# A four-layer transformer kernel: two late weight tiles placed elsewhere, a tile split at another place, and the first attention units and token halves taken in another order

## The reference

```python
def hybrid_layer(x, ...):                       # twice
    h = rms_norm(x, norm_mix)
    proj = h @ w_in                             # queries, keys, values of four mixers, gates
    ys = [nsa_mixer(...), stick_breaking_mixer(...), gla_mixer(...), forgetting_mixer(...)]
    branch = jnp.einsum('bsnc,ncd->bsnd', ys, w_branch)
    mixed = jnp.sum(gates * branch, axis=2)
    x = x + mixed @ w_out
    return x + jnp.square(jax.nn.relu(rms_norm(x, norm_ff) @ w_ff1)) @ w_ff2

def second_block(x, c, ctx, c_ctx, ...):
    for i in range(2):                          # i = 0: GQA, 512 tokens; i = 1: MLA, 256 tokens
        sh_a, sc_a, g_a, sh_m, sc_m, g_m = split(silu(c) @ w_ada[i] + b_ada[i], 6)   # and for c_ctx
        y = mixer_i(x * (1 + sc_a) + sh_a, ...)          # 16 heads, softmax attention
        x = layer_norm(alpha * x + g_a * y, ...)
        x = layer_norm(alpha * x + g_m * sq_relu_mlp(x * (1 + sc_m) + sh_m, w1, w2), ...)
```

## Time and profile before

| | |
|---|---|
| three runs | 2367.37, 2374.55 and 2376.17 us; median 2374.55 |
| profiled execution | 2367.38 us, of which 2365.6 us are the span from first to last instruction |
| mean granted clock | 0.979 |
| TensorE busy | 2235.9 us, 95% of the span |
| VectorE, ScalarE, GpSimd busy | 1239.0, 691.1 and 479.0 us |
| TensorE not busy | 129.7 us of the span (2365.6 - 2235.9) |

### The profile page before, as it was taken

One profiled execution on the slowest core, in us unless ns is written; L12 is line 12 of the kernel. 1 busy time (PEld: TensorE's weight loads), 2 busy tenths in 40 slices (PEclk: granted clock), 3 DMA queues, 4 the chain that ended last, 5 costly groups with the idle time before them and its releaser, 6 DMA issues.

```text
span 2365.6 us, 33139 instructions
## 1 busy us (share of the span) xinstructions
PE 2235.9 (95%) x13928; PEld 1805.5 (76%) x13928; DVE 1239.0 (52%) x1689; ACT 691.1 (29%) x1530; POOL 479.0 (20%) x259
## 2 busy tenths in 40 slices
PE   7999999999999999999999897889999998998998
PEld 7998788799888977887998644447888884555887
DVE  5675436764445744367653226664443443465666
ACT  2224453122012244532220357522112112262211
POOL 2221112243312211122432000101111110102332
PEclk9999999999999999999999898999999999999999
DMA  7634665564365355655646311022223222202551
GB/s 229 215 136 149 215 250 161 189 231 186 125 183 215 108 183 215 245 161 201 226 179 214 110 47 42 1 71 89 84 95 107 73 81 87 88 26 77 197 197 65
DMA packets 210120, 340.13 MB, mean 144 GB/s; under 512 B 46475, under 2 KB 78198, under 8 KB 209846
## 3 DMA queue, kind: packets, MB, share of 16 engines
q1 hardware_dynamic: 208880, 334.50, 40.8%
q0 software_dynamic: 944, 3.47, 0.4%
q10 hardware_dynamic: 150, 0.04, 0.0%
HBM read 335.90 MB, written 2.10 MB: 143 GB/s over the span
## 4 chain that ended last, share of the span: by engine, by line
PE 57%; ACT 4%; DVE 3%; issue 1%; DVEq 0%; ACTq 0%
PE bank L2057 15%; PE bank L268 13%; PE bank L270 12%; PE bank L269 12%; PE bank L635 3%; PE bank L2060 2%; ACT work L2378 1%; DVE ring_low L256 1%; ACT work L2294 1%; ACT work L1093 1%; DVE cos L2572 1%; PE bank L638 0%; ACT L1093 0%; ACT work L2303 0%; PE bank L928 0%
## 5 line engine op out<-in xcount | busy, mean ns | idle before, releaser
L269 PE MATMUL bank<-hT_high,ring_low 128*128 128x256 f32 (+1 forms) x2032 | 604.0, 297 | 0.0
L269 PEld LDWEIGHTS bank<-hT_high,ring_low 128*128 128x128 f32 x2032 | 387.8, 191 | 12.4 <-issue 0.5
L249 POOL CAST ring_high<-ring 128x2048 fp32r<-128x2048 f32 (+2 forms) x108 | 203.7, 1887 | 712.3 <-PE bank L270 649.8
L256 DVE TENSOR_TENSOR ring_low<-ring,ring_high 128x2048 fp32r<-128x2048 f32 (+2 forms) x108 | 239.0, 2215 | 131.8 <-POOL ring_high L249 131.6
L268 PE MATMUL bank<-hT_low,ring_high 128*128 128x256 f32 (+1 forms) x1008 | 293.5, 291 | 15.4 <-DVE ring_low L256 7.9
L270 PE MATMUL bank<-hT_high,ring_high 128*128 128x256 f32 (+1 forms) x1008 | 285.7, 283 | 0.0
L249 POOL CAST half_high<-ring 128x2048 fp32r<-128x2048 f32 x64 | 128.6, 2013 | 675.4 <-PE bank L270 469.9
L268 PE MATMUL bank<-ring_low,hidden_high 128*128 128x512 f32 x640 | 254.0, 397 | 0.0
L1093 ACT ACTIVATE work<-bank 128x512 f32<-128x512 f32 (+10 forms) x268 | 121.3, 476 | 377.7 <-PE bank L270 320.1
L268 PEld LDWEIGHTS bank<-hT_low,ring_high 128*128 128x128 f32 (+1 forms) x1008 | 190.6, 189 | 26.5 <-issue 17.0
L256 DVE TENSOR_TENSOR ring_low<-ring,half_high 128x2048 fp32r<-128x2048 f32 x64 | 152.7, 2391 | 99.7 <-POOL half_high L249 99.2
(11 more groups left out here) (236 smaller groups left out, 4482.0 us busy)
## 6 DMA issues: line engine op xcount, KB each, us to landing
ring<-w_ff SPq DMA_DIRECT2D x32, 2048.0 KB, 8.0
ring<-mlp_w SPq DMA_DIRECT2D x32, 2048.0 KB, 7.9
ring<-w_in SPq DMA_DIRECT2D x30, 2048.0 KB, 8.1
ring<-w_ada SPq DMA_DIRECT2D x24, 2048.0 KB, 7.7
ring<-w_branch SPq DMA_DIRECT2D x24, 512.0 KB, 6.2
ring<-w_in SPq DMA_DIRECT2D x32, 256.0 KB, 4.2
ring<-w_out SPq DMA_DIRECT2D x4, 2048.0 KB, 7.5
ring<-gqa_w_qkv SPq DMA_DIRECT2D x3, 2048.0 KB, 7.7
```

The lines of the kernel that those rows point to most:

```text
L249: nc.gpsimd.tensor_copy(self.high(i), self.part(i, False)).then_inc(self.high_made, 1)
L256: nc.vector.tensor_tensor(self.part(i, True), self.part(i, False), self.high(i).bitcast(F32), ALU.subtract)\
L269: nc.tensor.matmul(out, a[1], b[0], start=False, stop=False)
```

## The change

It has six parts. No arithmetic is added or removed; the products, their operands and their sizes stay, except that the first two `up` chunks of the GQA layer are taken as two halves of 256 tokens.

```diff
+    late_tiles = Carver(gates.rearrange("p a b -> p (a b)")).take(2, KD, 512)
...
-    tiles += [ada_tile(n) for n in ada_late]
...
-    slots += [0, 2, 1, 0, 2, 1, 0, 2]
-    feed = [1, 3, 0, 2]
-    slots += [feed[n % N_SLOTS] for n in range(len(tiles) - len(slots))]
-    W = Weights(sem, "w", chip["ring"], slots, tiles, prev.held, {"up1": done("wo11")})
+    slots += [0, 2, 1, 0, 2, 1]
+    slots += [0, 2, 1, 3, 0, 2, 3, 1, 0, 3, 2, 1, 0, 3, 2, 1]
+    W = Weights(sem, "w", chip["ring"], slots, tiles, prev.held, {"up3": done("wo11")})
...
-        W.load(sp, back_at)
+        W.load(sp, back_at, W.order["up0"] + 1)
+        sp.wait_ge(mixed_whole, KD // 2)
+        for at, n in enumerate(ada_late):
+            sp.dma_start(late_tiles[:, at], w_ada[:, :, 512 * n:512 * n + 512]).then_inc(wk1_in, 16)
+        W.load(sp, W.order["up1"])
...
         Y.make_low(nc, dve, OUT_CUT + 3)
+        X.make_low(nc, dve, 0, 1)
         add_out(1, 0)
         norm(0, TT + 1, xn)
         add_out(1, 1)
         norm(1, TT + 2, xn)
         for c in range(2):
             low_bits("yT", ROW_FF, hT_high[1], c)
-        X.make_low(nc, dve, 0, 1, 2, 3)
+        X.make_low(nc, dve, 2, 3)
```

```diff
-    tiles = [*q_tiles, cmp_tile, in_tile("kwg", KS0 + 256, 280, "vwg"), in_tile("kvs", KS0, 256, "vs"),
+    tiles = [*q_tiles, cmp_tile, kk_tile, vv_tile,
...
         if l > 0:
-            Y.make_low(nc, dve, 0, 1)
+            Y.make_low(nc, dve, 0)
```

The copy of `fc`. ACT takes it between the two tiles of the GLA output:

```diff
         for t in range(TT):
+            if t == 1:
+                ps = PROJ.arrived(act, "fc")
+                copy(fox_row[0:8, :], ps[0:8, 0:S]).then_inc(PROJ.free("fc"), 1)
             ps = OT.arrived(act, f"go{t}")
...
-        ps = PROJ.arrived(act, "fc")
-        copy(fox_row[0:8, :], ps[0:8, 0:S]).then_inc(PROJ.free("fc"), 1)
```

Attention start. `a9`, its square mean and the last two inverse roots, scalings and rotations go into the first units of attention (n counts units):

```diff
+                if i == 0 and n == 0:
+                    project(NORMED - 1, last_q)
+                    square_mean(NORMED - 2, OT)
+                    swap(NORMED - 3)
...
+                if i == 0 and n == 0:
+                    take_q(NORMED - 1)
+                    deviation(NORMED - 2, OT)
+                if i == 0 and n == 1:
+                    deviation(NORMED - 1, OT)
...
+                if i == 0 and n == 1:
+                    rotate_q(NORMED - 3)
+                    scale_q(NORMED - 2)
+                if i == 0 and n == 3:
+                    scale_q(NORMED - 1)
+                if i == 0 and n == 5:
+                    rotate_q(NORMED - 2)
+                if i == 0 and n == 7:
+                    rotate_q(NORMED - 1)
```

Output product and token halves. The first output product of each layer of the second block (`wo00`) is taken chunk by chunk inside the last units, in an SC bank; in the GQA layer the first two `up` chunks are taken for tokens 0 to 255 while the last tile's norm runs, and that tile's transposes use PT banks:

```diff
+                left = PAIRS * U + LAG[i] - n
+                if 1 <= left <= U:
+                    parts = {2: (0, 3, 6), 3: (0, 2, 4, 6)}[U]
+                    out_part(i, 0, 0, first_out, range(*parts[U - left:U - left + 2]))
...
+                        if i == 0 and t == NT[0]:
+                            pe.wait_ge(hT_cut, TT)
+                            half_ups = [PROJ.claim(pe, f"0up0_{n}") for n in range(2)]
+                            for n, ps in enumerate(half_ups):
+                                up_part(0, 0, n, ps[:, 0:S], slice(0, S))
                         pe.wait_ge(x_ready, ln_count[i, 0, t - 1])
```

More of the change, by code:

```diff
@@ L720, in tensor @@
         ps = PROJ.claim(pe, "kskw")
-        gemm_T(ps[:, S:2 * S], Y.arrived(pe, "kwg", 0), slice(0, P))
-        w = Y.arrived(pe, "kvs", 0)
-        gemm_T(ps[:, 0:S], w, slice(0, P)).then_inc(PROJ.full, 1)
+        w = Y.arrived(pe, "kk", 0)
+        for i in range(2):
+            last = gemm_T(ps[:, i * S:(i + 1) * S], w, slice(i * P, i * P + P))
+        last.then_inc(PROJ.full, 1)
         ps = PROJ.claim(pe, "vs")
+        w = Y.arrived(pe, "vv", 0)
         for t in range(TT):
-            last = gemm(ps[:, t * P:(t + 1) * P], w, slice(P, 2 * P), t)
+            last = gemm(ps[:, t * P:(t + 1) * P], w, slice(0, P), t)
         last.then_inc(PROJ.full, 1)
-        w = Y.arrived(pe, "kwg", P)
+        w = Y.arrived(pe, "vv", P)
         ps = PROJ.claim(pe, "vwg")
@@ L1848, in second_block @@
     early, spare = Carver(hT.rearrange("p a b -> p (a b)")), Carver(chip["work"], m.at - 7 * S)
-    m_prob = early.take(6, 512)
+    m_prob = [early.take(512) for _ in range(6)]
     m_turn = [early.take(4, S), z.rearrange("p a b -> p (a b)").rearrange("p (a b) -> p a b", a=4),
@@ L2184, in operands, with out_part, attention @@
             return m_qT[0:MLA_QK, h, :], m_kT[0:MLA_QK, h, :], m_v[:, :, h * HD:h * HD + HD]
-        def attention(i):
+        def out_part(i, t, h, ps, chunks):
+            yT = buffers(i)[2]
+            w = W.arrived(pe, f"{i}wo{h}")
+            for c in chunks:
+                last = mm(ps[:, :], yT[:, c, t * P:t * P + P], w[:, c, :], c == 0, c == KD - 1)
+            return last
+        def attention(i, last_q):
             prob, turned_p = buffers(i)[0:2]
@@ L2214, in attention @@
                         last.then_inc(PT.full, 1)
+                if i == 0 and n == LAG[i]:
+                    swap(NORMED - 1)
                 if n > LAG[i] and (n - LAG[i]) % U == 0:
@@ L2225, in attention, with up_part @@
                     last.then_inc(OT.full, 1)
+                    if c == PAIRS - 2:
+                        first_out = SC.claim(pe, f"{i}wo00")
+                        OT.taken(pe, f"{i}o{PAIRS - 3}")
+                left = PAIRS * U + LAG[i] - n
+                if 1 <= left <= U:
+                    parts = {2: (0, 3, 6), 3: (0, 2, 4, 6)}[U]
+                    out_part(i, 0, 0, first_out, range(*parts[U - left:U - left + 2]))
+            return first_out
+        def up_part(i, q, c, ps, tokens, wait=False):
+            w = X.arrived(pe, f"{i}up{q}{c // 4}", c // 2 % 2)
+            cols = slice(c % 2 * P, c % 2 * P + P)
+            for at, k in enumerate((4, 5, 6, 7, 0, 1, 2, 3)):
+                if wait and at in (0, 2, 4):
+                    pe.wait_ge(hT_cut, cut_base[i] + NT[i] + at // 2)
+                last = product(nc, ps, [part[:, k, cols] for part in w],
+                               [part[:, k, tokens] for part in (hT_high, hT_low)], at == 0, at == KD - 1)
+            return last
@@ L2241, in tensor @@
-            w = [W.arrived(pe, f"{i}wo{h}") for h in range(2)]
+            first_out = attention(i, last_q)
+            for c in range(PAIRS - 2, PAIRS):
+                OT.taken(pe, f"{i}o{c}")
+                last = out_part(i, 0, 0, first_out, [c])
+            last.then_inc(SC.full, 1)
             for t in range(NT[i] + 1):
                 for h in range(2):
-                    if t < NT[i]:
-                        ps = OT.claim(pe, f"{i}wo{t}{h}")
-                        for c in range(KD):
-                            last = mm(ps[:, :], yT[:, c, t * P:t * P + P], w[h][:, c, :], c == 0, c == KD - 1)
-                        last.then_inc(OT.full, 1)
-                    if t >= 1 and h == 0:
+                    if t < NT[i] and t + h > 0:
+                        out_part(i, t, h, OT.claim(pe, f"{i}wo{t}{h}"), range(KD)).then_inc(OT.full, 1)
+                    if t >= 1 and h == 0:
+                        if i == 0 and t == NT[0]:
[3 more added lines that the diff above has]
+                                up_part(0, 0, n, ps[:, 0:S], slice(0, S))
@@ L2304, in modulate @@
                          scale=mod_col(i, part + 1, k, t // TT), bias=mod_col(i, part, k, t // TT))
-            last.then_inc(PROJ.free(name), 1)
+            last.then_inc(banks.free(name), 1)
         def take_gate(i, kind, s):
```

197 lines of the change are left out of this document (117 added, 80 removed).

## The result

The changed kernel takes 2357.16 us (median of 8 runs, 2356.63 to 2360.36) against 2376.93 (8 runs, 2367.37 to 2382.32). The ratio is 0.9929, 95% interval 0.9915 to 0.9943, which is 14 to 20 us less (17 by the ratio; the medians lie 19.8 apart). The forecast was 2352, range 2339 to 2364. The profiled execution took 2356.95 us.

The account below looks back on a forecast made before the run. TensorE, busy 2235.9 of 2365.6 us, was taken as the bound, with gains only in its waits. Terms 6.0 + 5.4 + 1.3 + 0.4 + 1.0 + 3.0 + 4.8 = 21.9 off 2374.55 gave 2352.6, range 2339 to 2364.

Parts of the forecast that it names:

- rival B: Attention start loses 2 us, feed-forward entries give 0 to 1, token halves their least: 11.6 us, about 2363; chance 0.18.
- A: Rival: feed-forward entries give full durations, half-speed stretches there and at `g1` go too: about 2342 us; chance 0.16.
- Part 1: Feed-forward entries of both layers: earlier tile load and two early low parts shorten TensorE's wait; 6.0 us, range 2 to 13.
- a shorter wait may keep the clock: Layer 0 feed-forward entry: reason to take 4 us, from 2.5 to 4.2, for the first chunk's earlier end.
- case without contention: Feed-forward entries: casts and low parts run side by side; 6.3 and 5 us of wait, 0.2 for clock, 11.5 together.
- Part 2: GLA output, both layers: ACT's `fc` copy ahead of four squares removes TensorE's 2.92 us wait; 5.4 us, range 2.8 to 9.
- hidden behind those 6.5 us: GLA output: the next reader of ACT's chain, late by 0.36 us, costs nothing behind `g1` and the modulation product.
- Part 3: Key tile and layer 1 entry: earlier `kvs` low part 1.3 us (-1.9 to 3.6); `q1` low part behind `low_bits` 0.4.
- Part 4: Attention start: exponentials of units 0 and 1 fill gaps around the inverse roots; 1.0 us, range -2 to +4.
- From there attention runs at its old pace: Attention start: the lead of 1.6 us or less at the unit after the fourth stays to the end.
- Part 5: Last attention units, GQA and MLA: chunks of `wo00` fill TensorE's short waits; 3.0 us (1.7 and 1.3), range 1 to 5.
- Part 6: GQA `up` start: 48 half-size matmuls run during the 3.92 us wait for the last tile's norm; 4.8 us, range 3 to 6.

Follow-up runs that it names:

- x_wo: Changed kernel with the product `wo00` again taken in one piece after attention's last unit: 2356.98 us, ratio 0.9929 to the kernel before.
- x_key: Changed kernel with tiles `kwg` and `kvs` in place of `kk` and `vv`, low parts' places kept: 2360.53 us, ratio 0.9932 to the kernel before.

## Why the prediction was right, and where its terms were not

**The total.** 21.9 us were forecast; the ratio gives 16.9 (14 to 20). Direction, size and range held, and rival B's 11.6 and A's 32 lie outside. The size is partly luck: most terms came out below the forecast, and undoing one part at a time gives 2.6 + 2.9 + 0.7 - 0.5 + 0.0 + 5.5 = 11.2, each with 5 to 6 us of doubt. The remaining 5.7 is inside that doubt and can't be given to a part (no run undid the moved low parts of `q1` and `cmp`).

**Part 1, 6.0 forecast, 2.6 by the runs (-3 to 8), 4.4 by the traces.** The mechanism was right row by row: low part 3.95, addition 464.04 for 465.0, the normalisation held to 468.8. That one with a single SBUF operand is held, too, stood in the forecast without a row for it, and the trace shows it (2.31). "I take 4" for layer 0 was the first chunk finished at 479.3 instead of 483.5, 26.1 us behind the start of `out1`'s product. Where the clock stays up in the entry it came out so (25.9 and 25.8 in `x_wo` and `x_key`); the failed step is "a shorter wait may keep the clock". In six of eight profiles the clock fell inside or behind the entry, and the mean is 28.0, about 2.7 less than before; in layer 1 it is 1.7 for the 2 forecast. The case without contention was mis-sized as well: the wait of layer 1 was 3.98 us, where 5 was given to it. The remedy followed from the forecast's own chain: one low part fits the 5.08 us, two don't.

**Part 2, 5.4 forecast; 5.3 by the traces, 2.9 (-1.8 to 7.6) by the runs.** The forecast let `g2` start 2.7 earlier, and each GLA stretch is 2.6 shorter. But only 1.0 of it is wait, since two new ones, 0.39 and 1.51, stand behind ACT at the next two products; 1.6 is the clock, which the forecast had kept at half for `g1`. So the step "hidden behind those 6.5 us" failed, and that the size is right is luck.

**Part 3, 1.3 and 0.4.** The wait of 1.59 is gone, as forecast; 0.7 by the runs, within noise. The larger tile isn't 2 MB, as the forecast has it, but two loads of 512 KB.

**Part 4, +1.0 forecast, about -1 by the traces.** The chain to the fourth unit came as forecast: the last root ended at 1423.54, which is 1432.7 less the 9.1 by which the kernel was ahead, and the exponentials followed at 1428.60, 2.8 ahead of the earlier trace rows on the same count. The step that failed is "From there attention runs at its old pace". TensorE, then ScalarE:

```profile
1427.32 1.08 PE L2095 MATMUL bank<-consts,work 128*128 128x128 f32 x4 [4.45 <-DVE work L2594]
...
1431.33 2.35 PE L2092 MATMUL bank<-work 128*128 128x256 f32 x4 [2.93 <-ACT work L2370]
...
1435.29 0.69 ACT L2459 ACTIVATE work<-bank,cos 128x512 f32<-128x512 f32 x1 [3.62 <-DVE cos L2662]
```

TensorE waits 4.45 us ahead of a transpose, since DVE was held at `scale_q(9)` by the last root, and the rotation of `a8`, which stands behind it in DVE's order, frees the bank only then (L2594, at 1426.75), and then 2.93 for ACT's copy behind the exponentials. The next unit's exponentials start at 1435.29; before it was 1443.81, or 1434.7 on the same count. The lead of 2.8 is gone within one unit.

**Part 5, 3.0 forecast, 0.0 by the runs (-5 to 5), -3.3 by the traces.** The two short waits were filled as forecast. The failed step is that nothing was asked about who reads the product: "fill these 1.62 us" priced TensorE's wait and not DVE's queue, where three low parts stood ahead of the addition. With them moved, the GQA stretch is 93.0 us, 2.0 less than without the part (95.0) for the 1.7 forecast; the MLA stretch is 67.4 and still longer than without it (65.9). Whether moving the low parts gains anything without part 5 wasn't run.

**Part 6, 4.8 forecast, 5.5 by the runs (0.4 to 10.5), 4.1 to 5.2 by the traces.** The second chunk is taken 16.8 us behind the end of the output products instead of 20.9, with a wait of 2.02 left for the modulation where 1.7 was forecast.

**The base.** The forecast set its sum against one profiled execution of 2367.38 and shifted it by 7.2 to the median. That was right, but for a reason that it didn't have: the difference is clock and not waits. With eight runs the median before is 2376.93, 2.4 us above the 2374.55 that it used.

## What to carry to other kernels

When a product is pulled forward, follow it to the instruction that reads it, and look at what stands ahead of that one on its in-order engine; here three 128x2048 low parts cost as much as the filled waits gave, and with them moved the kernel was 5.7 us faster, all of it in one of the two layers by the traces. Work moved into another engine's idle time has to be measured with its contention: the 5.08 us on VectorE held one low part (3.98) and not two (6.18), and the smaller move gained 4.5 us more (5.4 against no early low part, on the same chip). Take the worth of a removed wait from several executions, since one profile can be 10 us off the median by its clock alone.

## What the runs showed of the hardware that was not expected

The same program, with the same waits within 1 us, ran at a mean clock of 0.979 in one execution and 0.975 in another and took 9.8 us longer. The additional time at half clock (3.4 to 6.8 us each, at 114, 667, 766 and 831 us) stands in part where TensorE had been busy without a wait for over 10 us. A stretch of 3.4 us inside the entry of the feed-forward, present in some profiles of the same code and absent in others, moved TensorE's start from 22.8 to 24.7 us behind `out1`'s. A normalisation with a single SBUF tensor as its operand (128x1024, 0.75 us) took 2.31 us beside casts, as forecast, while an addition that reads a bank kept its 0.69.
